# The first third of layer 0's conditioning stands alone ahead of the first projection; the other thirds, layer 1's and the mLSTM's gates run beside that projection

## The reference, cut to what matters

```python
for l in range(DEPTH):                      # DEPTH = 2
    mod_lat = jnp.split((c_act @ ada_wl + ada_b[l])[:, None, :], 6, axis=-1)
    mod_ctx = jnp.split((cc_act @ ada_wl + ada_b[l])[None, None, :], 6, axis=-1)
    u_lat = h_lat * (1.0 + mod_lat[1]) + mod_lat[0]
    u_ctx = h_ctx * (1.0 + mod_ctx[1]) + mod_ctx[0]
    # layer 0: even_mixer (mLSTM and HGRN), layer 1: odd_mixer (Hyena and retention)
    h_lat = layer_norm(DEEPNORM_ALPHA * h_lat + mod_lat[2] * y_lat, ...)
    v_lat = h_lat * (1.0 + mod_lat[4]) + mod_lat[3]
    f_lat = moe_ffn(v_lat, ...)
    h_lat = layer_norm(DEEPNORM_ALPHA * h_lat + mod_lat[5] * f_lat, ...)
```

## Time and profile before

| what | us |
|---|---|
| median of 3 runs | 2463.77 |
| the profiled execution, its own time | 2451.74 |
| its span, first to last instruction | 2449.9 |
| start to the modulate stage | 0 to 85.3 |
| modulate stage | 85.3 to 97.3 |
| first projection | 97.3 to 182.5 |
| gates stage | 182.5 to 214.3 |
| mLSTM and its norm | 214.3 to 327.7 |
| second projection | 327.7 to 504.4 |

### The profile page before, as it was taken

How to read it: one execution, slowest core, us unless ns; L and a number is a source line. 1 busy time by engine, 2 the same in 40 slices (tenths; PEclk the granted TensorE clock), 3 DMA queues, 4 the chain that set the end, 5 groups by cost and what they waited for, 6 DMA issues and landing times. The chain is left out here.

```text
span 2449.9 us, 31472 instructions
## 1 busy us (share of the span) xinstructions
PE 1977.4 (81%) x10528; PEld 1017.6 (42%) x10529; DVE 854.2 (35%) x1752; ACT 236.7 (10%) x517; POOL 680.4 (28%) x967
## 2 busy tenths in 40 slices
PE   3795759935788899899999976959778988787795
PEld 0342523323446454455555433324455544344442
DVE  0004720057545333233333344554343322222224
ACT  1102110122002000000000011001110000000001
POOL 0000000021101566456666400000005654444440
PEclk8895679977897999999999987979879999999998
DMA  9400047300206699999899575121238999999944
GB/s 378 181 1 1 0 176 291 121 1 1 91 0 279 229 410 411 414 408 393 348 409 393 218 309 216 69 107 65 90 130 358 415 420 422 422 422 420 419 194 189
DMA packets 99974, 601.65 MB, mean 246 GB/s; under 512 B 23200, under 2 KB 23435, under 8 KB 40444
## 3 DMA queue, kind: packets, MB, share of 16 engines
q1 hardware_dynamic: 66012, 516.78, 51.5%
q0 software_dynamic: 33888, 83.86, 9.2%
HBM read 590.50 MB, written 51.92 MB: 262 GB/s over the span
## 5 line engine op out<-in xcount | busy, mean ns | idle before, releaser
L1609 PE MATMUL bank<-moe_w,blk_xT 128*64 128x256 f32 x5632 | 679.4, 396 | 2.7 <-DVE blk_xT L1685 2.7
L1609 PEld LDWEIGHTS bank<-moe_w,blk_xT 128*64 128x64 f32 x5632 | 404.4, 142 | 220.1 <-issue 32.2
L1620 PE MATMUL bank<-moe_w,xt 128*64 128x512 f32 x1408 | 332.1, 592 | 1.5 <-DVE xt L1697 1.5
L1536 POOL DMA_INDIRECT ada_rows<-v_tokens,blk_gidx x264 | 272.5, 1032 | 140.2 <-issue 135.1
L451 PE MATMUL bank<-w_in_ring,xt 128*128 128x512 f32 x544 | 241.7, 604 | 13.0 <-DMA w_in_ring<-in_odd_w_in 10.2
L1685 DVE STREAM_TRANSPOSE blk_xT<-ada_rows 128x512 f32<-128x512 f32 x132 | 94.0, 712 | 450.8 <-PE bank L1609 427.1
L1552 POOL DMA_INDIRECT y_rows<-xt,blk_sidx x176 | 179.9, 1022 | 94.6 <-issue 48.4
L1704 DVE COPY xt<-bank 128x512 f32<-128x512 f32 x176 | 121.8, 692 | 149.3 <-PE bank L1620 149.3
L451 PEld LDWEIGHTS bank<-w_in_ring,xt 128*128 128x128 f32 x544 | 104.3, 194 | 148.1 <-issue 137.5
L1620 PEld LDWEIGHTS bank<-moe_w,xt 128*64 128x64 f32 x1408 | 100.9, 137 | 127.5 <-issue 100.5
L1668 ACT ACTIVATE xt<-bank 128x128 f32<-128x128 f32 x174 | 48.3, 278 | 1046.7 <-PE bank L1609 1046.7
(11 more groups left out here) (386 smaller groups left out, 1746.4 us busy)
## 6 DMA issues: line engine op xcount, KB each, us to landing
moe_w<-in_experts SPq DMA_DIRECT2D x128, 3072.0 KB, 31.0
ada_ring<-in_ada_w SPq DMA_DIRECT2D x12, 2048.0 KB, 17.2
w_out<-in_ada_w POOLq DMA_DIRECT2D x12, 2048.0 KB, 8.8
moe_w<-y_rows SPq DMA_DIRECT2D x24, 1024.0 KB, 20.5
w_in_ring<-in_even_w_in SPq DMA_DIRECT2D x8, 2048.0 KB, 12.6
w_in_ring<-in_odd_w_in SPq DMA_DIRECT2D x7, 2048.0 KB, 19.2
ada_rows<-v_tokens,blk_gidx POOLq DMA_INDIRECT x264
w_out<-in_even_w_out SPq DMA_DIRECT2D x1, 4096.0 KB, 12.3
```

The costliest lines, as they stand in the source:

```text
L1536: pool.indirect_dma_start(came[q][:, u], None, v_quarters, bass.IndirectOffsetOnAxis(ap=gidx[q][:, u:u + 1], axis=0), bounds_check=4 * n_t ...
L1609: last = nc.tensor.matmul(g.bank[1][64 * h:64 * h + 64, 0:HID], xT[:, k], w[:, s, (2 * k + h) * HID:(2 * k + h + 1) * HID], start=k == 0, ...
L1620: last = nc.tensor.matmul(g.bank[3][64 * h:64 * h + 64, :], hT[:, 64 * m:64 * m + 64], w[:, s, at:at + 512], start=m == 0, stop=m == 1)
```

## The change

`load_stage` and `ada_rows_stage` become one `start_stage`. Only the first third of layer 0 is multiplied there. SP issues `c_cols`, the four pieces, then `base`, the biases of both layers and `h`. Layer 0's other two thirds, layer 1's three and the gates go into a new side, `FrontSide`, of the first projection; the outputs then go round 4 banks, and two empty slots stand behind the 12 outputs. The gate's row (entry 2) is spread at the start of the HGRN's norm stage and copied by ACT. The second projection has no side any more, and both `ada_columns_stage` calls and `gates_stage` are gone.

```diff
+def start_stage(g):
+        ada = AdaRows(g, [(0, 0)], [ring[:, i] for i in range(4)], (0, 1), [g.ada_rows[:, 0]])
+            @block.sync
+            def _(sp):
+                sp.dma_start(g.c_cols[:], g.dram["c_cols"]).then_inc(c_loaded, 16)
+                ada.load(sp)
+                sp.dma_start(g.base[:], g.dram["t_base"]).then_inc(table_loaded, 16)
+                sp.dma_start(g.ada_bias[:], g.dram["ada_b"].rearrange("l p c -> p l c")).then_inc(bias_loaded, 16)
+                sp.dma_start(g.h[:], g.dram["x_all"]).then_inc(h_loaded, 16)
+                sp.wait_ge(h_loaded, 16)
...
+class FrontSide:
+    TAIL = 2
+    BANKS = 4
+    GATE_BANK, TURN_BANK, ADA_BANKS = 4, 5, (6, 7)
...
+        ring = sb("ada_ring", [P, 2, 2 * 2048])
+        self.ada = AdaRows(g, [(0, 1), (0, 2), (1, 0), (1, 1), (1, 2)], [ring[:, i] for i in range(2)], self.ADA_BANKS,
+    def sync(self, sp):
+        sp.dma_start(self.wg[:], self.g.dram["w_gates"]).then_inc(self.loaded, 16)
+        sp.dma_start(self.gb[:], self.g.dram["gate_b"]).then_inc(self.loaded, 16)
+    def load(self, pool):
+        pool.memset(self.spare, 0.0).then_inc(self.zeroed, 1)
+        self.ada.load(pool)
+    def pe(self, pe, n):
+        if n == 1:
+            pe.wait_ge(self.loaded, 32)
...
+        if n == 6:
+            pe.wait_ge(self.step, self.n_rows)
...
+        if 5 <= n <= 13 and n % 2 == 1:
+            self.ada.turn(pe, (n - 5) // 2, self.TURN_BANK)
+        if 2 <= n < 12:
+            for i in range(2):
+                self.ada.multiply(pe, 2 * (n - 2) + i)
...
 def norm_stage(...)
             def _(act):
+                if rows:
+                    act.wait_ge(row_ready, 1)
+                    for v in range(2):
+                        for half in range(2):
+                            nc.scalar.activation(g.mod_row[:, v, half * 512:(half + 1) * 512], g.bank[4 + 2 * v + half][:], ACT.Copy).then_inc(row_copied, 1)
                 act.wait_ge(step, marks["var"])
                 nc.scalar.activation(st[:, 1], st[:, 1], ACT.Sqrt).then_inc(rooted, 1)
             def _(pe):
+                if rows:
+                    mod_rows(g, *rows).then_inc(row_ready, 1)
                 pe.wait_ge(step, marks["gated"])
...
-                (7, "N", allt, lambda j: hg[:, j], "silu")], lambda _: AdaRows(g, 1, work, 2, (6, 7)))
-            ada_columns_stage(g, 1)
+                (7, "N", allt, lambda j: hg[:, j], "silu")])
```

More of the change, by code:

```diff
@@ L208, with __init__, load @@
-class AdaRows:
[L213 to L225, removed]
-    def multiply(self, pe, n):
[L228 to L232, removed]
+class AdaRows:
+    PER_GROUP = 4
+    def __init__(self, g, work, slots, banks, rows):
+        self.g, self.slots, self.banks, self.rows = g, slots, banks, rows
+        self.work = work
+        self.pieces = [(i, l, group, part) for i, (l, group) in enumerate(work) for part in range(self.PER_GROUP)]
+        self.loaded = [new_sem(g, "ada_w_loaded") for _ in slots]
+        self.used, self.copied, self.turned, self.added = (new_sem(g, x) for x in ("ada_w_used", "ada_rows_copied", "ada_turned", "ada_added"))
+        self.adds = []
+    def load(self, eng):
+        for n, (i, l, group, part) in enumerate(self.pieces):
+            if n >= len(self.slots):
+                eng.wait_ge(self.used, n - len(self.slots) + 1)
+            at = n % len(self.slots)
+            eng.dma_start(self.slots[at].rearrange("p (k c) -> p k c", k=2), self.g.dram["ada_w"][l, group, part]).then_inc(self.loaded[at], 16)
+    def multiply(self, pe, n):
+        i, l, group, part = self.pieces[n]
+        at = n % len(self.slots)
+        pe.wait_ge(self.loaded[at], 16 * (n // len(self.slots) + 1))
+        if part == 0 and i >= 2:
+            pe.wait_ge(self.copied, 4 * (i - 1))
+        bank = self.g.bank[self.banks[i % 2]]
+        weights = self.slots[at].rearrange("p (k c) -> p k c", k=2)
@@ L257, in act, with turn @@
[L257 to L268, removed]
+    def turn(self, pe, i, bank):
+        pe.wait_ge(self.copied, 4 * (i + 1))
+        if i:
+            pe.wait_ge(self.added, 2 * i)
+        for c in range(4):
+            last = self.g.nc.tensor.transpose(self.g.bank[bank][:, c * P:(c + 1) * P], self.rows[i % len(self.rows)][:, c * P:(c + 1) * P], self.g.ident)
+        last.then_inc(self.turned, 1)
@@ L278, in _ @@
+            def _(pool):
+                pool.memset(g.zero_row[:], 0.0).then_inc(zeroed, 1)
+                pool.memset(g.ada_rows[:], 0.0).then_inc(zeroed, 1)
+                pool.wait_ge(zeroed, 2)
+            @block.scalar
+            def _(act):
+                act.wait_ge(c_loaded, 16)
+                nc.scalar.activation(g.c_act[:], g.c_cols[:], ACT.Silu).then_inc(act_done, 1)
+                act.wait_ge(zeroed, 2)
+                ada.copy(act, 0)
             @block.tensor
             def _(pe):
-                for n in range(rows.PIECES):
-                    rows.multiply(pe, n)
@@ L283, in _ @@
[L283 to L298, removed]
-            @block.tensor
-            def _(pe):
-                for group in range(3):
-                    for c in range(4):
-                        last = nc.tensor.transpose(g.bank[group][:, c * P:(c + 1) * P], g.ada_rows[:, group, c * P:(c + 1) * P], g.ident)
-                    last.then_inc(turned, 1)
+                pe.wait_ge(act_done, 1)
@@ L318, in _, with mod_rows @@
-                for which in (1, 4):
-                    part = mods[:, which * KT:(which + 1) * KT, :]
-                    link(nc.vector.tensor_scalar(part, part, 1.0, None, ALU.add))
+                ada.add(dve, 0, 2)
+def mod_rows(g, l, which):
+    for v in range(2):
+        for k in range(KT):
+            col = g.mods[:, l, which * KT + k, v:v + 1].broadcast_to([P, P])
+            last = g.nc.tensor.matmul(g.bank[4 + 2 * v + k // 4][:, (k % 4) * P:(k % 4 + 1) * P], col, g.ident,
+                                      start=True, stop=True)
+    return last
@@ L344, in _ @@
                 last.then_inc(turned, 1)
[L346 to L351 removed]
+            if rows is not None:
+                mod_rows(g, l, rows).then_inc(row_ready, 1)
         @block.scalar
```

272 lines of the change are left out of this document (137 added, 135 removed).

## The result

The changed kernel takes 2441.19 us (median of 4 runs, 2438.94 to 2443.50), the kernel before in the same session 2464.89 us (4 runs, 2463.47 to 2467.29). The ratio is 0.9911, 95% interval 0.9892 to 0.9930: 22 us faster by the ratio, 23.7 by the medians. The forecast was 2426 us, with 2440 as the upper end of its range: the time came out just above it. The direction held, and so did most of the terms; of the 37.2 us that were worked out, 13.5 are missing by the medians.

What follows compares the result with a forecast made beforehand. The front was taken as bound by conditioning-matrix loads, both projections by PE. Terms -53.5 - 2.8 + 45.2 - 25.8 - 3.2 + 2.9 = -37.2 us took 2463.8 to 2426.6 us; range 2410 to 2440.

Steps and rivals of the forecast that it cites:

- the mixtures of experts: Both mixture stages, whose code the change leaves alone: no term in the sum, so a change of 0 us.
- the size of the first projection: First projection with the gates, 117.0 us before, would take 162.2 us: plus 45.2 us, 35 to 51.
- The front and the modulate stage: Start to issue of the input weights: minus 53.5 us; from there to the projection's first matmul: minus 2.8 us.
- the wait for `w_gates`: First projection, ahead of the gates' matmuls: PE waits 8.9 us for their weights, 6 to 11.
- M+26: Assumed landing of the gates' weights, 26 us after M, the issue of the input weights; bounds M+23 and M+28.
- The ring: First projection: PE waits for pieces reloaded through two slots, 14 us in sum; 9 to 17.
- The end: Behind the first projection's last output: copies, last turn and two adds start the mLSTM stage 3.9 us later.
- 20 pieces: First projection: the pieces' multiplications cost PE 2.03 us each, 40.6 us in all.
- rival 3: First projection: waits lower PE's clock, so gates and next output run at half speed; plus 8 to 12, 2436; chance 0.13.
- The second projection: 12 pieces leave (24.4 us) and first weights stop sharing (1.4): minus 25.8 us; layer 1's columns stage goes: minus 3.2.
- the HGRN's norm: ACT's copies of the gate's row and its table load make the root late: plus 2.9 us, 2 to 5.
- Rival 5: First projection: POOL's two loads go one after the other, ring waits cost 57 us instead of 14; 2470; chance 0.03.

Runs made afterwards that it cites:

- the pair on one chip: The kernel before and the changed kernel, both unedited, run again on one chip: 2459.08 us before, 2437.80 us changed, ratio 0.9919.

## Why the prediction was right, and where it failed

**The step that failed: the mixtures of experts stand in the sum at nothing, without a reason.** The forecast took them as left alone, since their code is. The new resident tile `ada_bias` moves every tile allocated behind it by 384 bytes, and with that the loads of the second mixture fall from 420 to 412 GB/s. That is +8.9 us in the pair on one chip, +9.3 with an unused tile of that size alone, and -9 when 128 bytes restore the place. None of the rivals had it. It is about 9 of the 13.5 to 16 us that are missing by the medians, and 9 us less than 2441.19 would have been inside the range.

**The rest that is missing is the size of the first projection**: +50.2 us in the one pair and +54.5 in the other against +45.2. The pair on one chip flatters the sum. Its two profiles differ by 26.3 us, and by 35.2 without the term of the tile, but that execution of the changed kernel was its quickest; with the biases padded the kernel is 28 us faster than before by the ratio, still 9 short of 37.2. In that profile it takes 177.8 us from the issue of the input weights to the mLSTM stage, 49 to 50 more than in the two profiles of before, where +45.2 - 2.8 = +42.4 was worked out.

**The front and the modulate stage** were right to 1.0 us: pieces at 9.7, 14.5, 19.4 and 24.3 us as listed, the weights issued at 32.8 and 32.2 against 31.8.

**The first projection** was worked out at 162.2 us and took 165.8 in one profile, 171.6 in the other. Its terms one by one: the wait for `w_gates` was taken in the middle of its two bounds, M+26, and came at the late bound, M+28.0 and M+27.6. With the first output quick (7.1 us) PE waits 11.6 us instead of the 8.9 of the sum, with it slow (10.2 us) 8.9. The Trainium skill's rule that was named for it (DMA: Bandwidth & Descriptors, Queues, rings and completion order: turns between queues) gave that late landing, M+28; the trace agrees with 27.6 and 28.0. The ring was 14.5 and 16.1 against 14, its single waits up to 2.9 and 3.0 us where 2.9 was worked out; three slots and one piece per output both take it away. With the 6.8 us for a load that follow from the Trainium skill (DMA: Bandwidth & Descriptors, Anatomy of one DMA) as an estimate the ring would have cost 4: the trace's 8.8 was the one to use. The end was right to 0.2 us. One size was off the other way, and by luck: 20 pieces were put at 40.6 us by 2.03 each, but two in a row take 3.55 (75.47 to 79.02 above), some 36 in all; the outputs beside them take 7.0 to 7.1 us instead of 6.87, which gives back 2. Without that luck the term would have missed by 2 to 3 us more.

**The clock** was rival 3, and part of it came, in the profile of 171.6 us. In the profile of 165.8 us every piece takes 1.90 and the mean clock is 0.97; in that of 171.6 four pieces behind waits take 2.6 to 3.4, three outputs 7.25 to 8.10 and the first output 10.2, at a clock of 0.91. It is the same code, with less waiting in the slower one, so it is the clock that makes these 6 us between executions; the windows from the first matmul to the mLSTM stage:

```profile
41.05:206.84 165.79, 134.17 (x612) 47.03 (x612) 19.90 (x33) 23.92 (x36) 12.30 (x21) 0.97 0.70 274
```
```profile
41.71:213.27 171.56, 143.95 (x612) 49.28 (x612) 19.90 (x33) 23.94 (x36) 12.25 (x21) 0.91 0.68 264
```

The argument against it, that single waits under 3 us would leave the clock alone, failed: in the slower profile, and with the gates early, the pieces at the lower clock stand behind waits of 2.2 to 3.7 us. But waits of up to 3.0 us in the other profile left it at its upper level, so a wait is not enough by itself. What else decides was not tried.

**The second projection** (-30.6 for -29.0) and **the HGRN's norm** (+2.4 for +2.9) were nearly right. The first weights of the former gain 2.7 us (11.9 to 9.2) and not 1.4 when POOL's loads are gone; the copies on ACT are shown as the cause of the latter. Rival 5, loads that go one after the other, is out: no wait for a piece is over 3.0 us in the changed kernel.

**Open.** The residual stage took 1.5 us more than before on the same chip, and 3 us more in the first pair; it was not followed. The mLSTM stage with its norm varies from 107 to 114 us over the profiles.

## What to carry to other kernels

Before costing a change at nothing for the stages that it leaves alone, list what it allocates: a tile whose size is no multiple of 256 bytes shifts everything behind it, and a stage that is bound by its loads pays 2% if the tile that they fill stops beginning on a multiple of 256 bytes. Pad resident tiles so that the large load targets stay aligned. Take more than one profile before a sum of stages is compared with it: one execution here was 9 us under its median. A ring that must deliver two pieces per step needs three slots if a load takes longer than the step leaves it; a small load that PE will wait for goes ahead of the large ones in its queue; and work gains by moving only from a place where it was waited for. Layer 0's pieces left a front bound by its loads; layer 1's went from one projection in which PE is full to another, and moving them back is worth 14 us.

## What the runs showed of the hardware

- The rate of large loads depends on the start of the target in the partition. From 100 to 500 us behind the start of the second mixture it is 420 or 421 GB/s in the six profiles whose tile begins on a multiple of 256 bytes and 412 in the seven others (128 beyond one); from 100 to 250 us behind the start of the first, 419 in three and 410 or 411 in ten (64 or 192 beyond one).
- The first mixture of experts runs at one of two paces, in both kernels: 667 to 670 us in four profiles, 673 to 680 us in the others. In its quick profiles ACT's silu starts 0.2 us behind the end of the matmuls that feed it, block after block; in the slow ones there are stretches of blocks with a lag of some 1.0 us. The profile of the changed kernel, and that with the row's copies moved, which has the same code in this stage (a matmul behind the ones ACT waits for, then ACT):

```profile
1101.03 1.89 PE L1660 MATMUL bank<-moe_w,xt 128*64 128x512 f32 x8
1102.05 0.28 ACT L1708 ACTIVATE xt<-bank 128x128 f32<-128x128 f32 x1 [6.10 <-PE bank L1649]
```
```profile
1103.61 1.89 PE L1660 MATMUL bank<-moe_w,xt 128*64 128x512 f32 x8
1103.82 0.28 ACT L1708 ACTIVATE xt<-bank 128x128 f32<-128x128 f32 x1 [5.30 <-PE bank L1649]
```

  With the long lag PE waits for DVE's product (38 times, 12.2 us in sum, in the first of these two profiles), in the second never. It is where the first pair of profiles lost 11 us in that mixture: the profile of before was a quick one, 12 us under its own median. What sets the lag stays open.
- PE's wait of 9 to 12 us ahead of the gates also makes the gates themselves slower, 8.6 to 9.4 us in the eight profiles that have it instead of 7.05 in the two without. The kernel before has 8.39 us behind a wait of 2.80.
